# A two-block layer on one core: GpSimd sums the conv results, one product with ones gives the mean, and the normalisation of branch b is spread over three blocks of branch a

## The reference

```python
u = jax.nn.glu(glu_in, axis=-1)
u = causal_depthwise_conv(u, w_dw[i]) + b_dw[i]              # 31 taps, one filter for each channel
u = jax.nn.silu(layernorm(u, ln_g[i], ln_b[i])) * jax.nn.silu(z_b)
y_b = u @ w_br_b[i]
...
y_a = o_a @ w_br_a[i]
gate_a, gate_b = jnp.split(jax.nn.sigmoid(gate_logits + b_gate[i]), N_BRANCHES, axis=-1)
mixed = (gate_a * y_a + gate_b * y_b) @ w_out[i]

def layernorm(x, g, b):
    mu = jnp.mean(xf, axis=-1, keepdims=True)
    var = jnp.mean(jnp.square(xf - mu), axis=-1, keepdims=True)
    y = (xf - mu) * lax.rsqrt(var + EPS)
    return y * g + b
```

## Time and profile before

| what | us |
|---|---|
| median of 3 runs | 2235.69 |
| lowest and highest | 2234.68, 2239.55 |
| profiled execution, its own time | 2236.06 |
| span of the profiled execution | 2234.2 |
| TensorE busy | 2151.8 (96%) |
| VectorE busy | 1494.3 (67%) |
| ScalarE busy | 1224.1 (55%) |
| GpSimd busy | 262.7 (12%) |

### The profile page before, as it was taken

How to read it: one execution, slowest core, us unless ns; L and a number is a source line. 1 busy time by engine, 2 the same in 40 slices (tenths; PEclk the granted TensorE clock), 3 DMA queues, 4 the chain that set the end, 5 groups by cost and what they waited for, 6 DMA issues and landing times.

```text
span 2234.2 us, 29331 instructions
## 1 busy us (share of the span) xinstructions
PE 2151.8 (96%) x10062; PEld 1775.3 (79%) x10062; DVE 1494.3 (67%) x2779; ACT 1224.1 (55%) x2356; POOL 262.7 (12%) x385
## 2 busy tenths in 40 slices
PE   7999999999999999999999999999999899999996
PEld 5788888887777778888788887788788688888885
DVE  4778778788999876655765565653466654456665
ACT  4666666676666754445555555544354355555542
POOL 0111111144433431010000000000000000000000
PEclk9999999999999999999999999999999999999998
DMA  5866766778767686665656555565555455654452
GB/s 183 243 196 197 206 195 195 206 195 234 213 185 196 171 253 202 203 214 201 217 197 246 205 206 176 189 209 171 188 185 170 141 190 185 199 161 146 153 206 94
DMA packets 440112, 431.30 MB, mean 193 GB/s; under 512 B 37888, under 2 KB 313488, under 8 KB 438464
## 3 DMA queue, kind: packets, MB, share of 16 engines
q1 hardware_dynamic: 424208, 381.69, 54.9%
q0 software_dynamic: 5920, 26.68, 3.5%
q10 hardware_dynamic: 9872, 21.50, 2.5%
HBM read 406.72 MB, written 23.09 MB: 192 GB/s over the span
## 4 chain that ended last, share of the span: by engine, by line
PE 77%; DVE 13%; SPq 3%; DMA 3%; issue 2%; ACT 2%; POOL 1%; DVEq 0%; ACTq 0%; POOLq 0%
PE pair L439 22%; PE pair L441 22%; PE pair L440 22%; DVE w_lo L419 4%; DVE QB L1018 3%; DMA conv_and_gate<-ubz 2%; SPq L387 1%; PE QA L1412 1%; PE RA L1428 1%; SPq L693 1%; PE RA L586 1%; SPq L654 1%; PE QB L1497 0%; PE QA L1063 0%; DVE o_t L906 0%
## 5 line engine op out<-in xcount | busy, mean ns | idle before, releaser
L419 DVE TENSOR_TENSOR w_lo<-raw,w_hi 128x512 fp32r<-128x512 f32 x1376 | 932.0, 696 | 434.8 <-ACT w_hi L413 432.8
L413 ACT ACTIVATE w_hi<-raw 128x512 fp32r<-128x512 f32 x1376 | 836.5, 626 | 502.9 <-PE pair L441 479.3
L439 PE MATMUL pair<-w_hi,in_hi 128*128 128x512 f32 x2368 | 953.1, 402 | 8.3 <-DVE in_lo L1082 4.2
L441 PE MATMUL pair<-w_hi,in_lo 128*128 128x512 f32 x2368 | 927.6, 392 | 0.0
L440 PE MATMUL pair<-w_lo,in_hi 128*128 128x512 f32 x2368 | 925.7, 391 | 0.0
L439 PEld LDWEIGHTS pair<-w_hi,in_hi 128*128 128x128 f32 x2368 | 447.4, 189 | 98.2 <-DVE in_lo L1082 5.1
L441 PEld LDWEIGHTS pair<-w_hi,in_lo 128*128 128x128 f32 x2368 | 446.7, 189 | 95.9
L440 PEld LDWEIGHTS pair<-w_lo,in_hi 128*128 128x128 f32 x2368 | 447.7, 189 | 88.9 <-issue 1.0
L987 POOL TENSOR_TENSOR acc_p<-acc_p,tap 128x256 f32<-128x256 f32 x128 | 130.3, 1018 | 51.2 <-ACT tap L971 43.8
L1018 DVE SCALAR_TENSOR_TENSOR QB<-upad,cwl,QB 128x256 f32<-128x256 f32 x304 | 133.6, 479 | 0.0
L971 ACT ACTIVATE tap<-upad,cwl 128x256 f32<-128x256 f32 x160 | 79.9, 499 | 13.5 <-POOL acc_p L987 12.8
(11 more groups left out here) (396 smaller groups left out, 1781.1 us busy)
## 6 DMA issues: line engine op xcount, KB each, us to landing
raw<-in_w_in_dram SPq DMA_DIRECT2D x512, 256.0 KB, 3.7
raw<-in_w_in_dram SPq DMA_DIRECT2D x80, 1024.0 KB, 5.1
raw<-in_w_out_dram SPq DMA_DIRECT2D x48, 1024.0 KB, 5.0
raw<-in_w_kv_shared_dram SPq DMA_DIRECT2D x24, 1024.0 KB, 4.9
raw<-in_w_br_a_dram SPq DMA_DIRECT2D x16, 1024.0 KB, 5.8
raw<-in_w_br_b_dram SPq DMA_DIRECT2D x16, 1024.0 KB, 5.6
raw<-in_w_mem_kv_dram SPq DMA_DIRECT2D x16, 1024.0 KB, 4.9
raw<-in_w_ple_gate_dram SPq DMA_DIRECT2D x16, 1024.0 KB, 5.0
```

Of the source, the lines that this page charges most:

```text
L413: act.activation(w_hi[:, u % 2, q % UK], raw[:, u, q % UK], ACT.Copy).then_inc(hi_ready[u], 1)
L419: dve.tensor_tensor(w_lo[:, u % 2, q % UK], raw[:, u, q % UK], w_hi[:, u % 2, q % UK].bitcast(F32), ALU.subtract)\
L439: pe.matmul(o, xh, wh, start=(q == 0), stop=False)
L441: mm = pe.matmul(o, xl, wh, start=False, stop=(q == KC - 1))
```

## The change

1. GpSimd keeps a running sum `usum` of the 16 conv results. The addition for group j-1 stands in group j's part of GpSimd's stream, behind the two copies of filter taps (L978, L979) and ahead of the first addition of taps. The last one stands behind the first part of the delta rule. DVE waits for the addition of the group before the last before it writes the same `ubz` buffer again.
2. The mean takes one product of ones with `usum`, in Y0 at hs 14. The 16 products with `ub` are gone.
3. The steps of the normalisation are given by tables, counted from Y0: centring at 34, 38, 56, 60 (Y1 hs 2, 6, 24, 28), products of squares four half-steps behind each, square root at 66, reciprocal at 67 (Y2 hs 2 and 3), and the four chunks at 70, 82, 94, 106, so 12 half-steps apart. Before, counted the same way, they were: mean 66 to 69, centring 71 to 77, squares 74 to 80, square root 82, reciprocal 82, chunks at 84, 92, 100, 108, so 8 half-steps apart. Inside a chunk the distances stay.
4. The reloads are waited for half by half, and the first half of `zb` is loaded one block earlier.

```diff
+    def add_u_pool(pool, j, par):
+        pool.wait_ge(s["u_ready"], j + 1)
+        if isinstance(j, int) and j == 0:
+            pool.tensor_copy(usum[:, :], ubz[:, par, 1]).then_inc(s["u_added"], 1)
+        else:
+            pool.wait_ge(s["u_added"], j)
+            pool.tensor_tensor(usum[:, :], usum[:, :], ubz[:, par, 1], ALU.add).then_inc(s["u_added"], 1)
...
-        reach(pool, s["u_ready"], j)
+        if not isinstance(j, int) or j > 0:
+            add_u_pool(pool, j - 1, 1 - par)
...
+            reach(dve, s["u_added"], j - 1)
             dve.tensor_tensor(ubz[:, par, 1], taps_sum[:, S:2 * S], acc[:, :], ALU.add)\
...
-    LN0 = 32 * (BLK_Y + 2 - BLK_GB)
+    LN0 = 32 * (BLK_Y - BLK_GB)
+    MEAN_AT, CENTRE_AT, RSTD_AT, SCALE_AT = 14, (34, 38, 56, 60), 67, (70, 82, 94, 106)
...
-        if 2 <= at < 6:
-            c = at - 2
-            if c == 0:
-                pe.wait_ge(s["ubz_loaded"], 32)
-            for j in range(4 * c, 4 * c + 4):
-                mm = pe.matmul(QA[:, 0:S], ones, ub[:, j], start=(j == 0), stop=(j == KC - 1))
...
+        if at == MEAN_AT:
+            pe.wait_ge(s["u_added"], KC)
+            pe.wait_ge(s["oa_lo_done"], 2 * NG)
+            pe.matmul(QA[:, 0:S], ones, usum[:, :], start=True, stop=True).then_inc(s["var_done"], 1)
+        if at - 4 in CENTRE_AT:
...
         for g in range(NG):
             rule_pool(pool, g)
+            if g == 0:
+                add_u_pool(pool, KC - 1, (KC - 1) % 2)
...
         reload(ub, 1, 0)
         pool.wait_ge(psum_free, BLK_Y + 1)
         gate_a(2)
+        after(ubz_loaded=16)
         reload(ub, 1, 1)
+        after(ubz_loaded=32)
+        reload(zb, 0, 0)
         pool.wait_ge(psum_free, BLK_Y + 2)
         gate_a(3)
-        after(ubz_loaded=32)
-        for c in range(2):
-            reload(zb, 0, c)
+        after(ubz_loaded=48)
+        reload(zb, 0, 1)
```

More of the change, by code:

```diff
@@ L306, in program @@
     orn = sb("orn", [P, TT * GROUP])
+    usum = sb("usum", [P, S])
     assert spot[0] <= nc.sbuf_usable_end
@@ L354, in program @@
              "bg_loaded", "gate_biased", "b_tanh", "glu_ready", "gate_a_stored", "b_cols", "b_cols_taken", "cwl_staged",
-             "pool_taps", "u_summed", "u_ready", "ubz_stored", "ubz_loaded", "gb_stored", )
+             "pool_taps", "u_summed", "u_ready", "u_added", "ubz_stored", "ubz_loaded", "gb_stored", )
     s = {n: sem(n) for n in names}
@@ L1283, in program @@
     X_TURNS = {BLK_MEM_V0: (0, TURN_X1), BLK_MEM1: (1, TURN_X2)}
-    LN0 = 32 * (BLK_Y + 2 - BLK_GB)
+    LN0 = 32 * (BLK_Y - BLK_GB)
+    MEAN_AT, CENTRE_AT, RSTD_AT, SCALE_AT = 14, (34, 38, 56, 60), 67, (70, 82, 94, 106)
     def norm_b_pe(pe, at):
         at -= LN0
-        if 2 <= at < 6:
-            c = at - 2
-            if c == 0:
-                pe.wait_ge(s["ubz_loaded"], 32)
-            for j in range(4 * c, 4 * c + 4):
-                mm = pe.matmul(QA[:, 0:S], ones, ub[:, j], start=(j == 0), stop=(j == KC - 1))
[L1296 to L1299, removed]
+        if at == MEAN_AT:
[3 more added lines that the diff above has]
+        if at - 4 in CENTRE_AT:
+            c = CENTRE_AT.index(at - 4)
             pe.wait_ge(s["squared"], c + 1)
@@ L1306, in norm_b_act @@
         at -= LN0
-        if at == 6:
+        if at == MEAN_AT + 1:
             act.wait_ge(s["var_done"], 1)
             act.activation(mub[:, :], QA[:, 0:S], ACT.Copy, scale=1.0 / D).then_inc(s["mean_ready"], 1)
-        if 8 <= at < 16 and at % 2 == 0:
-            c = (at - 8) // 2
+        if at - 2 in CENTRE_AT:
+            c = CENTRE_AT.index(at - 2)
             act.wait_ge(s["centred"], c + 1)
@@ L1314, in norm_b_act @@
             act.activation(sqb[:, c % 2], ub[:, 4 * c:4 * c + 4], ACT.Square).then_inc(s["squared"], 1)
-        if at == 18:
+        if at == RSTD_AT - 1:
             act.wait_ge(s["var_done"], 5)
             act.activation(rsb[:, :], QB[:, 0:S], ACT.Sqrt, scale=1.0 / D, bias=eps_col[:, :]).then_inc(s["mean_ready"], 1)
-        if at >= 22 and (at - 22) % 8 == 0 and at < 22 + 32:
-            c = (at - 22) // 8
+        if at - 2 in SCALE_AT:
+            c = SCALE_AT.index(at - 2)
             act.wait_ge(s["ln_scaled"], c + 1)
@@ L1324, in norm_b_act @@
             ins.then_inc(s["ln_affine"], 1)
-        if at >= 24 and (at - 24) % 8 == 0 and at < 24 + 32:
-            c = (at - 24) // 8
+        if at - 4 in SCALE_AT:
+            c = SCALE_AT.index(at - 4)
             act.wait_ge(s["ln_affine"], c + 1)
@@ L1329, in norm_b_act @@
             act.activation(sqb[:, c % 2], ub[:, 4 * c:4 * c + 4], ACT.Tanh, scale=0.5).then_inc(s["ln_tanh"], 1)
-        if at >= 30 and (at - 30) % 8 == 0 and at < 30 + 32:
-            c = (at - 30) // 8
+        if at - 10 in SCALE_AT:
+            c = SCALE_AT.index(at - 10)
             act.wait_ge(s["ln_gated"], c + 1)
@@ L1336, in norm_b_dve @@
         at -= LN0
-        if 7 <= at < 15 and at % 2 == 1:
-            c = (at - 7) // 2
+        if at in CENTRE_AT:
+            c = CENTRE_AT.index(at)
             dve.wait_ge(s["mean_ready"], 1)
+            dve.wait_ge(s["ubz_loaded"], 16 * (c // 2 + 1))
             dve.tensor_tensor(ub[:, 4 * c:4 * c + 4], ub[:, 4 * c:4 * c + 4], row(mub[:, :]), ALU.subtract)\
                .then_inc(s["centred"], 1)
-        if at == 18:
+        if at == RSTD_AT:
             dve.wait_ge(s["mean_ready"], 2)
             dve.reciprocal(rsb[:, :], rsb[:, :]).then_inc(s["rstd_ready"], 1)
-        if at >= 20 and (at - 20) % 8 == 0 and at < 20 + 32:
-            c = (at - 20) // 8
+        if at in SCALE_AT:
+            c = SCALE_AT.index(at)
             dve.wait_ge(s["rstd_ready"], 1)
@@ L1349, in norm_b_dve @@
                .then_inc(s["ln_scaled"], 1)
-        if at >= 26 and (at - 26) % 8 == 0 and at < 26 + 32:
-            c = (at - 26) // 8
+        if at - 6 in SCALE_AT:
+            c = SCALE_AT.index(at - 6)
             x = ub[:, 4 * c:4 * c + 4]
@@ L1354, in norm_b_dve @@
             dve.scalar_tensor_tensor(four(x), four(sqb[:, c % 2]), 1.0, four(x), ALU.add, ALU.mult).then_inc(s["ln_silu"], 1)
-        if at >= 28 and (at - 28) % 8 == 0 and at < 28 + 32:
-            c = (at - 28) // 8
+        if at - 8 in SCALE_AT:
+            c = SCALE_AT.index(at - 8)
             x = ub[:, 4 * c:4 * c + 4]
             dve.wait_ge(s["ln_silu"], c + 1)
-            dve.wait_ge(s["ubz_loaded"], 64)
+            dve.wait_ge(s["ubz_loaded"], 16 * (c // 2 + 3))
             dve.tensor_tensor(x, x, zb[:, 4 * c:4 * c + 4], ALU.mult).then_inc(s["ln_gated"], 1)
-        if at >= 32 and (at - 32) % 8 == 0 and at < 32 + 32:
-            c = (at - 32) // 8
+        if at - 12 in SCALE_AT:
+            c = SCALE_AT.index(at - 12)
             dve.wait_ge(s["ub_hi_done"], c + 1)
```

## The result

| what | us |
|---|---|
| before, median of 4 runs | 2236.58 (2234.68 to 2239.55) |
| after, median of 4 runs | 2221.44 (2219.57 to 2223.59) |
| after : before | 0.9931, interval 0.9919 to 0.9943 |
| profiled execution after, its span | 2221.26, 2219.4 |

The account below looks back on a forecast made before the run. TensorE (PE), busy 96% of the span, was taken as the bound. From the profiled 2236.06 us, -6.5 (mean) -6.9 (Y3) -1.8 (clock) +0.8 (groups) = -14.4 gave 2221.7, stated as 2222; range 2218 to 2230.

Parts of the forecast that it names:

- Part 1: Mean: 16 products with ones go and one comes, 15 x 0.435 = 6.5 us less on PE, no new wait.
- Part 2: Normalisation chunks 12 half-steps apart: DVE's lead lasts, margin 0.7 us; 0.3 of Y3's 7.16 us excess stays, bounds 0 to 3.5.
- rival B: Chunks in Y3: lead used up earlier, 3.5 us of stalls and the clock fall remain, 2226.7 us; chance 0.17.
- Part 3: Clock in Y4: with PE unbroken in Y3, the 1.79 us excess goes; bounds 0 and 1.79.
- Part 4: Centring and squares moved into Y1 and Y2's start: no wait of PE, taken at 0, bounds 0 and 1 us.
- Part 5: Group blocks: 16 GpSimd additions delay DVE by up to 0.5 us each, mostly covered; cost 0.8 us, bounds 0 and 7.8.
- Rival C: Group blocks: exclusion hits `bproj` or the store's cover is too small, 0.52 us longer each, 2228.7 us; chance 0.12.
- rival D: Group blocks: PE's longer wait makes its clock fall there; slower, 2252 us with ten further falls; chance 0.05.
- Part 6: Reloads: no transfer added, first half of `zb` asked for near 1010 instead of 1021.6; taken at 0.
- Rival E: No gain: PE's wait only moves, for example to the square root or reloaded halves; 2232 to 2236 us; chance 0.06.
- rival A: The forecast itself: mean, Y3 and clock savings come about, groups cost at most 3 us; 2219 to 2225; chance 0.60.

Follow-up runs that it names:

- The two variants with 8 half-steps: The kernel after with only the chunk places changed: 70, 78, 86, 94 took 2225.26 us; 84, 92, 100, 108 took 2229.5 us.
- the early variant: The kernel after with the chunks at 70, 78, 86, 94, so 8 half-steps apart instead of 12: 2225.26 us, ratio 0.9945.
- the mean alone: The kernel before with only GpSimd's additions and one product for the mean, at half-step 5 of Y2, normalisation as before: 2230.26 us; again, 2231.49 us.
- the late chunks: The kernel after with the chunks back at 84, 92, 100, 108; mean, centring and squares stay early: 2229.5 us, ratio 0.9963.
- the three variants of its additions: The kernel after with GpSimd's group additions removed (2220.44 us), each done twice (2220.49 us), or made to wait until `glu` is ready (2221.98 us).
- the two kernels with the squares on GpSimd: The kernel after with GpSimd adding each chunk's four squares, 4 products instead of 16: 2216.99 us; the same with other places and an earlier reload: 2219.38 us.

## Why the prediction was right

**Part 1, the mean: right.** Forecast -6.5, measured -6.5 over Y0 to Y2, and -6.49 in Y2 when it is done alone. Y1 came out at 26.98 (27.0 expected) and Y2 at 23.50 (23.5).

**Part 2, the chunks: right, a little too careful.** Forecast -6.9 with 0.3 us left, measured -7.2 with nothing left. The working behind it can be read off the trace. The scalings start at 1032.08, 1042.42, 1051.34 and 1060.69, 28.6 us from first to last (28.5 expected); the last low part ends 38.8 us behind the first scaling (38.6), and PE reaches Y4 after 39.3 (39.3). The margin was 0.56 us (0.7). The eviction of Y2's result to `mixf`, 1.2 us of DVE's work at the start of its part of Y3, was booked at 0.5 and cost 0.43: the chunk with it has a period of 9.35 us, the one without it 8.92, so most of it fell into time that DVE would have waited. The two variants with 8 half-steps show that rival B was a matter of the distance and the lead, as Part 2 says, and what it would have cost: 3.9 us of stalls and 2225.26 us in all. That the last digit came out so well owes something to luck: the same account missed the stall of the early variant by 1.9 us.

**Part 3, the clock: the size right, the cause put too strongly.** Y4 lost 1.8 us as forecast. But "I put this fall down to the gaps of PE in Y3" is only half of it. Five traced executions had several waits in Y3 and one of 1.8 us for the last `ub_lo` at Y4's start: the kernel before twice, the mean alone twice, the late chunks. The fall came in four of them. With the early chunks, where PE also lost 3.9 us but had one long wait only and none at Y4's start, it did not. Without long waits it never came: not in the kernel after, its repeat, the three variants of its additions, nor in the two kernels with the squares on GpSimd, in which PE idled for less than 0.2 us in Y3. So the waits make the fall possible and do not decide it, and 1.8 us is the gain in an execution that would have had it. Whether the wait at Y4's start is what matters among them was not tested. The Trainium skill, "TensorE: Matmul & The Clock Gate", section "The HAM clock gate (the "warmup" mystery)", ties the half rate to idleness; the trace agrees in the direction, but two executions of one kernel with the same waits, of at most 1.83 us each, came out on either side.

**Part 4, the centring and the squares: right.** Y1 holds its 96 and 12 further products and nothing else, 26.98 us against 21.76 + 12 x 0.435 = 26.98.

**Part 5, the additions: the mechanism right, the size not measurable.** Forecast +0.8. The exclusion is there (1.22 us for a `w_lo` of 0.68 us). The Trainium skill, "SBUF — State Buffer", section "Who interferes with whom", says that a VectorE instruction with two inputs in SBUF and a GpSimd instruction that reads SBUF exclude each other. The trace after agrees at all eight additions beside which such an instruction of DVE began and overlapped by more than 0.1 us, and it holds the other way too: behind a `w_lo` or a `bproj` the addition itself takes longer (last section). What the group blocks make of it is about 1 us in their sum, if anything, and with each addition doubled they were no longer than without any. The prediction named the wait for the store as the cover. A nearer one it did not name: ahead of `glu` DVE had 0.3 us of idle time for ACT's tanh in each group, which took up most of the delay in the group shown. Rival C (7.8 us) falls, although the exclusion did hit `bproj` in two groups, as C feared. So does rival D. The prediction counted two group blocks with a fall of the clock before; the last one, 29.98 us at 0.89, makes three. In the trace after there were five, but five as well in the repeat of the kernel before and in the kernel without additions, with twelve group blocks of 297.4 and 297.0 us. The number of falls is scatter and not the additions' doing.

**Part 6, the reloads: right.** PE, ACT and DVE waited for no load of `ub` or `zb` in Y1 to Y3. Rival E falls with it.

**The sum.** -14.4 forecast, -14.8 measured between the two profiled executions, and 2236.58 - 2221.44 = 15.1 between the medians. That it agrees to half a microsecond is in part luck, since executions of one kernel lie 4 to 5 us apart and the fall of the clock might not have been there. One slip: the range 2218 to 2230 is said to leave out the edge of rival A, but it holds all of A, 2219 to 2225.

**What stays open.** Whether the additions cost the group blocks nothing or about 1 us: kernels that differ by that much can't be separated here, since the group blocks' sum alone went from 296.0 to 301.2 us among kernels that all had one addition, and the first group block began anywhere from 429.3 to 431.5 us, ahead of every edit. And what decides, between two executions with equal waits, whether the clock falls was not found.

## What to carry to other kernels

An engine that feeds the bound engine has a lead, and it can be kept like an account: work per period against the time in which the other engine uses it up. Four chunks with a deficit of 0.75 us each fit inside a lead of 6.7; with a deficit of 2.4 they did not, though the work was the same. Count every chunk, the last one too: leaving it out made one forecast here 1.9 us too small. When a chain fits only in part, give it both an earlier start and a longer distance, and test them one by one: here the start was worth 1.8 us and the distance behind it 3.9.

A sum over tiles that goes through products with ones costs the bound engine one product for each tile. Let an idle engine add the tiles up, and take one product: 0.435 us for each product saved. That worked twice here, in full for the mean and with 4.1 of 5.2 us for the squares. Before calling the idle engine's work free, look at the instruction of the neighbour that runs beside it, and at what idle time stands behind that.

Don't book a fall of the clock that follows waits as a sure gain; trace the kernel more than once.

## What the runs showed of the hardware

- **The exclusion goes both ways, and the later one pays.** The same addition of 128x256, 15 times in the kernel after, took from 0.717 to 1.114 us:

```profile
L982 POOL TENSOR_TENSOR usum<-usum,ubz x15: 717/900/1114, 501.4 to 863.2; 128x256 f32<-128x256 f32 x15
```

  It took 0.72 to 0.74 us in the six places where no instruction of DVE with two inputs in SBUF was under way when it began, 0.90 to 0.92 in the six where a `bproj` of 0.46 us had begun 0.14 us before, and 1.11 in the three where a `w_lo` of 0.68 us had begun 0.16 us before. In the other direction, a `w_lo` that began 0.24 us behind an addition of 0.90 us took 1.21 instead of 0.68. Each time the later one lost 0.13 or 0.14 us less than what was left of the earlier one.

  An addition of 128x512 took 1.73 and 2.31 us in Y1, beside DVE's pieces. Timeline of GpSimd in the kernel with the squares on it:

```profile
1004.03 2.31 POOL L1316 TENSOR_TENSOR sqb<-sqb 128x512 f32<-128x512 f32 x1 [1.03 <-ACT sqb L1329]
1006.42 1.06 POOL L1318 TENSOR_TENSOR sqb<-sqb 128x256 f32<-128x256 f32 x1
1007.45 1.73 POOL L1316 TENSOR_TENSOR sqb<-sqb 128x512 f32<-128x512 f32 x1
```

- **Equal waits, unequal clock.** Two executions of one kernel, with waits of 1.20, 0.19, 1.20 and 1.83 us in 17 us that were the same within 0.02 us, showed 1.00 and 0.93 in the block behind them, 21.90 and 23.51 us.
- **Single group blocks can't be compared.** Those of j = 4 to 15 were from 22.2 to 31.6 us long, and long and short ones changed places from one trace to the next, while the sum of twelve stayed within 296.0 and 301.2. Only the sum can be compared.
